# SSD scan with its decays spread over partitions by DMA and joined by predicated copies

## The reference, cut to what matters

```python
cs = jnp.cumsum(dtg * a_neg.astype(f32).reshape(g, r), axis=2)
decay = jnp.exp(jnp.where(causal, cs[:, :, :, None] - cs[:, :, None, :], -jnp.inf))
cb = jnp.einsum("bcign,bcjgn->bcijg", cg, bg)
xdt = dtg[..., None] * xg
y_diag = jnp.einsum("bcijgr,bcjgrp->bcigrp", cb[..., None] * decay, xdt)
y_off = jnp.einsum("bcign,bcgrpn->bcigrp", cg, starts) * jnp.exp(cs)[..., None]
...
y = y_f + y_b[:, ::-1] + lw["ssd_d"][:, None] * xs
```

## Time and profile before

| | |
|---|---|
| median of 3 runs | 3470.36 us (3469.86 to 3471.82) |
| profiled execution, its own time | 3470.05 us |
| its span | 3468.3 us |
| TensorE matmul busy | 3334.0 us (96%) |
| VectorE, ScalarE, GpSimd busy | 1618.2 (47%), 1262.5 (36%), 575.9 us (17%) |
| DMA | 212.96 MB, mean 61 GB/s |
| granted TensorE clock, mean | 0.985 |

### The profile page before, as it was taken

How to read it: one execution, slowest core, us unless ns; L and a number is a source line. 1 busy time by engine, 2 the same in 40 slices (tenths; PEclk the granted TensorE clock), 3 DMA queues, 4 the chain that set the end, 5 groups by cost and what they waited for, 6 DMA issues and landing times. The chain is left out here.

```text
span 3468.3 us, 55579 instructions
## 1 busy us (share of the span) xinstructions
PE 3334.0 (96%) x19856; PEld 3184.6 (92%) x19856; DVE 1618.2 (47%) x2846; ACT 1262.5 (36%) x2383; POOL 575.9 (17%) x703
## 2 busy tenths in 40 slices
PE   7879999999999999999999999899989999999997
PEld 2379999999999999999999998899988999999997
DVE  2373665745736657458366442344334222322233
ACT  4434444545355445443454443221233111110112
POOL 0002332421423324214223240000110000000000
PEclk9999999999999999999999999999999999999998
DMA  8311111111111111111111123443321111111111
GB/s 316 122 31 26 56 43 31 46 43 34 42 43 56 43 28 48 43 33 40 46 51 39 32 83 100 146 137 100 86 71 37 42 43 43 42 42 42 43 35 74
DMA packets 284847, 212.96 MB, mean 61 GB/s; under 512 B 10152, under 2 KB 266576, under 8 KB 284624
## 3 DMA queue, kind: packets, MB, share of 16 engines
q1 hardware_dynamic: 239808, 159.74, 15.3%
q10 hardware_dynamic: 44816, 50.35, 4.8%
HBM read 173.87 MB, written 36.18 MB: 61 GB/s over the span
## 5 line engine op out<-in xcount | busy, mean ns | idle before, releaser
L675 PE MATMUL bank<-h_hi,w_hi 128*128 128x384 f32 (+1 forms) x2520 | 876.7, 348 | 42.0 <-DVE z_t L1290 19.1
L675 PE MATMUL bank<-h_hi,w_lo 128*128 128x384 f32 (+1 forms) x2520 | 846.3, 336 | 0.0
L675 PE MATMUL bank<-h_lo,w_hi 128*128 128x384 f32 (+1 forms) x2520 | 846.3, 336 | 0.0
L1832 PE MATMUL bank<-a_hi,v_hi 128*128 128x384 f32 x1440 | 491.1, 341 | 31.7 <-DVE v_lo L1933 11.9
L675 PEld LDWEIGHTS bank<-h_hi,w_hi 128*128 128x128 f32 (+1 forms) x2520 | 474.4, 188 | 50.4 <-DVE z_t L1290 19.5
L1832 PE MATMUL bank<-a_lo,v_hi 128*128 128x384 f32 x1440 | 485.8, 337 | 0.0
L1832 PE MATMUL bank<-a_hi,v_lo 128*128 128x384 f32 x1440 | 485.7, 337 | 0.0
L675 PEld LDWEIGHTS bank<-h_lo,w_hi 128*128 128x128 f32 (+1 forms) x2520 | 474.7, 188 | 3.6
L675 PEld LDWEIGHTS bank<-h_hi,w_lo 128*128 128x128 f32 (+1 forms) x2520 | 473.5, 188 | 1.2
L1656 POOL TENSOR_TENSOR kq<-kq,fg 128x384 f32<-128x384 f32 x288 | 283.3, 1014 | 435.9 <-PE bank L807 434.6
L1832 PEld LDWEIGHTS bank<-a_hi,v_hi 128*128 128x128 f32 x1440 | 273.4, 190 | 46.8 <-issue 34.7
(11 more groups left out here) (253 smaller groups left out, 4655.3 us busy)
## 6 DMA issues: line engine op xcount, KB each, us to landing
raw<-in_w_in SPq DMA_DIRECT2D x104, 512.0 KB, 3.9
raw<-in_ffn_w SPq DMA_DIRECT2D x60, 512.0 KB, 3.7
ada<-in_ada_w SPq DMA_DIRECT2D x12, 2048.0 KB, 9.3
small<-gate_scratch ACTq DMA_DIRECT2D x72, 192.0 KB, 2.4
gate_scratch<-th ACTq DMA_DIRECT2D x48, 192.0 KB, 1.9
y_scratch<-x_t SPq DMA_DIRECT2D x8, 1152.0 KB, 4.4
small<-y_scratch ACTq DMA_DIRECT2D x48, 192.0 KB, 2.5
raw<-in_w_ssd_out SPq DMA_DIRECT2D x16, 512.0 KB, 4.0
```

The costliest lines, as they stand in the source:

```text
L675: last = pe.matmul(out, w[i][:, k, 0:cols_n], h[:, k, blk(hb)], start=(k == 0 and j == 0), stop=(k == KT - 1 and j == 2))
L1832: last = pe.matmul(banks[3 * s + b][:, 0:BW], wp[s][:, k, :], operand[ap][:, k, blk(b)], start=(k == 0 and j == 0), stop=(k == kt - 1 and ...
```

## The change

The cumulated decays go once, in the prologue, to a scratch in DRAM (18 stores). Per chunk SP loads the eight rows of the group, 4 KB, into all 128 partitions of `cumb` (three buffers). VectorE caps each row at the partition's own cumulated value (`min`), so that the masked side can't overflow; ScalarE makes the exponentials in place; VectorE copies the backward direction over the forward one where the mask says so, and the sum of the two directions' dt on the diagonal, and multiplies by C B straight from the bank. TensorE's decay arguments and GpSimd's sum go. x and B are turned once: `xb` holds all nine chunks. The dt factor's logarithm stays in the bias, the subtraction of `cum` moves to GpSimd per group, exp(cum) to ScalarE per group and into the evacuation of `dec`. Two weight tiles of the next group are loaded ahead of the HGRN state's store, one behind. In the diff "..." marks what is left out.

```diff
+        cum_dram = nc.dram_tensor("cum_scratch", [G, NC, 2, HPG, P], F32, kind="Internal").ap()
...
-        xb = [sb(f"xb{i}", [P, 512], F32, ssd_scope) for i in range(4)]
+        xb = sb("xb", [P, NC, BW], F32, ssd_scope)
         xp = sb("xp", [P, 2, GW], F32, ssd_scope)
         t_off = sb("t_off", [P, 512], F32, ssd_scope)
         y_tok = t_off[:, 0:GW]
-        me = sb("me", [P, 2048], F32, ssd_scope)
-        mm = me[:, 0:1024].rearrange("p (e n) -> p e n", e=2)
-        ex = me[:, 1024:2048]
-        rstd = me[:, 2048 - T:2048]
+        mm = sb("mm", [P, 2, 512], F32, ssd_scope)
+        cumb = sb("cumb", [P, 3, 8 * P], F32, ssd_scope)
+        rstd = cumb[:, :, :].rearrange("p a n -> p (a n)")[:, 0:T]
...
+    reset = acc[1][:, :]
     dt_v, dt_a, dt_b, dt_c, dt_d, dt_e = f_t, g_t, kf_t, kb_t, q_t, s_t
-    cum = x_t[0:64, 0, :]
+    cum = g_t[0:64, :]
...
-            def stage_a(g, tiles):
-                for t in tiles:
-                    base, step = A_COLS[t]
-                    load(g, t, g * step + base)
+            def load_a(g, t):
+                base, step = A_COLS[t]
+                load(g, t, g * step + base)
+
+            def load_cum(g, c):
+
+                if c >= 3:
+                    sp.wait_ge(m_ready.sem, m_ready.at(g, c - 2))
+                src = cum_dram[g:g + 1, c] if isinstance(g, int) else cum_dram[bass.ds(g, 1), c]
+                sp.dma_start(cumb[:, c % 3, :], src.rearrange("a d h t -> a (d h t)").broadcast_to([P, 8 * P])
+                             ).then_inc(cum_in[c % 3], 16)
+
+            def stage_a(g):
+                for t in (2, 3, 4):
+                    load_a(g, t)
+                load_cum(g, 3)
+                load_a(g, 5)
+                for c in (4, 5, 6):
+                    load_cum(g, c)
...
+                if t == 4:
+                    sp.wait_ge(cum_done, 1)
+                    for d in range(2):
+                        for c in range(NC):
+                            sp.dma_start(cum_dram[:, c, d], cum[32 * d:32 * d + 32, chunk(c)]).then_inc(cum_stored, 16)
...
+            sp.wait_ge(cum_stored, 16 * 2 * NC)
+            for c in range(3):
+                load_cum(0, c)
+            load_a(0, 0)
+            load_a(0, 1)
+
             with sp.Fori(0, G - 1) as g:
-                stage_a(g, late)
+                stage_a(g)
                 for t, (base, step) in enumerate(B_COLS):
+                    if t == 1:
+                        load_cum(g, 7)
+                        load_cum(g, 8)
                     if t == 3:
                         stores(g, False)
+                        for c in range(3):
+                            load_cum(g + 1, c)
                     load(g, 6 + t, g * step + (base + step))
+                load_a(g + 1, 0)
+                load_a(g + 1, 1)
                 store_h(g)
-                stage_a(g + 1, early)
...
-            def turn_xb(c, bank, with_cb):
+            def turn_xb(c, bank):
                 for e in range(2):
-                    last = pe.transpose(bank[:, e * P:(e + 1) * P], x_t[:, e, chunk(c)], ident)
-                last = pe.transpose(bank[:, GW:GW + P], b_t[:, chunk(c)], ident)
-                if with_cb:
-                    last = pe.matmul(bank[:, GW + P:GW + 2 * P], b_t[:, chunk(c)], c_t[:, chunk(c)],
-                                     start=True, stop=True)
-                return last
+                    pe.transpose(bank[:, e * P:(e + 1) * P], x_t[:, e, chunk(c)], ident)
+                return pe.transpose(bank[:, GW:GW + P], b_t[:, chunk(c)], ident)
 
             def ssd(g, k):
                 if k == 0:
@@ -696,39 +726,28 @@
                     last.then_inc(tr_ready.sem, 1)
                 if k < NB:
                     pe.wait_ge(silu_done.sem, silu_done.at(g, k - 2))
-                if k < NA1P:
+                if k < 5:
 
                     if k > 0:
                         pe.wait_ge(tr_kept.sem, tr_kept.at(g, 2 * k + 1))
-                    turn_xb(8 - 2 * k, S[0], False).then_inc(tr_ready.sem, 1)
-                    if k < 3:
-                        turn_xb(7 - 2 * k, S[1], False).then_inc(tr_ready.sem, 1)
+                    turn_xb(8 - 2 * k, S[0]).then_inc(tr_ready.sem, 1)
+                    if k < 4:
+                        turn_xb(7 - 2 * k, S[1]).then_inc(tr_ready.sem, 1)
                 if 2 <= k < 2 + NA1P:
                     p = k - 2
                     pe.wait_ge(xp_ready.sem, xp_ready.at(g, p + 1))
                     if p > 0:
                         pe.wait_ge(ctb_used.sem, ctb_used.at(g, p))
                     for j in range(2 if p < 3 else 1):
-                        last = pe.matmul(S[2][:, j * GW:(j + 1) * GW], xb[2 * (p % 2) + j][:, GW:GW + P],
+                        last = pe.matmul(S[2][:, j * GW:(j + 1) * GW], xb[:, 8 - 2 * p - j, GW:GW + P],
                                          xp[:, j, :], start=True, stop=True)
                     last.then_inc(ctb_ready.sem, 1)
                 if 4 <= k < 4 + NC:
                     c = k - 4
-                    pe.wait_ge(tr_kept.sem, tr_kept.at(g, 8 + c))
-                    turn_xb(c, S[0], True).then_inc(tr_ready.sem, 1)
-                    if c > 0:
-                        pe.wait_ge(exp_ready.sem, exp_ready.at(g, c))
-                    else:
-                        pe.wait_ge(sel_ready, g + 1)
-                    for d in range(2):
-                        pe.matmul(S[3 + d][:, :].rearrange("p (h i) -> p h i", i=P), id_bf[:, :],
-                                  neg_bf[d][:, :].rearrange("p (a i) -> p a i", a=1).broadcast_to([P, HPG, P]),
-                                  start=True, stop=False, skip_group_check=True)
-                        for h in range(HPG):
-                            last = pe.matmul(S[3 + d][:, h * P:(h + 1) * P], sel[:, d * HPG + h, :],
-                                             cum_hl[:, chunk(c)], start=False, stop=(h == HPG - 1),
-                                             skip_group_check=True)
-                    last.then_inc(arg_ready.sem, 1)
+                    if c >= 2:
+                        pe.wait_ge(m_ready.sem, m_ready.at(g, c - 1))
+                    pe.matmul(S[3 + c % 2][:, 0:P], b_t[:, chunk(c)], c_t[:, chunk(c)], start=True,
+                              stop=True).then_inc(cb_ready.sem, 1)
...
-            for a, src in enumerate((dt_d, dt_e, dt_b)):
+            for a, src in enumerate((dt_d, dt_e, cum)):
                 for c in range(NC):
                     i = a * NC + c
                     pe.transpose(S[i // 8][:, (i % 8) * 64:(i % 8 + 1) * 64], src[0:64, chunk(c)],
                                  ident[0:64, 0:64])
+            for c in range(NC):
+                pe.matmul(S[4][:, c * 32:(c + 1) * 32], dt_c[0:64, chunk(c)], cst[0:64, K_FOLD:K_FOLD + 32],
+                          start=True, stop=True)
             flat = v_tok[0:64, :, :].rearrange("p c t -> p (c t)")
-            for j in range(2):
-                last = pe.matmul(S[4 + j][:, 0:288], ones[0:64, :], flat[:, j * 288:(j + 1) * 288],
-                                 start=True, stop=True)
+            pe.matmul(S[3][:, 192:480], ones[0:64, :], flat[:, 0:288], start=True, stop=True)
+            last = pe.matmul(S[5][:, 0:288], ones[0:64, :], flat[:, 288:576], start=True, stop=True)
...
-                if 1 <= k < 1 + NA1P:
+                if 1 <= k < 6:
                     p = k - 1
-                    if p >= 2:
-                        wait(ctb_ready, g, p - 1)
-                    for j in range(2 if p < 3 else 1):
+                    for j in range(2 if p < 4 else 1):
                         wait(tr_ready, g, 2 + 2 * p + j)
-                        act.activation(xb[2 * (p % 2) + j][:, 0:BW], S[j][:, 0:BW],
-                                       ACT.Copy).then_inc(tr_kept.sem, 1)
+                        act.activation(xb[:, 8 - 2 * p - j, :], S[j][:, 0:BW], ACT.Copy).then_inc(tr_kept.sem, 1)
+                if k == 3:
+                    act.wait_ge(grp_ready, g + 1)
+                    act.activation(tok_g[:, 2, :, :], tok_g[:, 3, :, :], ACT.Exp)
                 if 5 <= k < 5 + NC:
                     c = k - 5
-                    wait(tr_ready, g, 9 + c)
-                    if c < 4:
-                        wait(ctb_ready, g, 3 if c < 2 else 4)
-                    else:
-                        wait(y_ready, g, c - 3)
-                    act.activation(xb[c % 4][:, :], S[0][:, :], ACT.Copy).then_inc(tr_kept.sem, 1)
-                    wait(arg_ready, g, c + 1)
-                    if c == 0:
-                        act.wait_ge(grp_ready, g + 1)
-                    else:
-                        wait(sum_ready, g, c)
-                    for d in range(2):
-                        for h in range(HPG):
-                            o = d * 512 + h * P
-                            last = act.activation(ex[:, o:o + P], S[3 + d][:, h * P:(h + 1) * P], ACT.Exp,
```

(74 more changed lines are left out.)

71 lines of the change are left out of this document (35 added, 36 removed).

## The result

| | before | after |
|---|---|---|
| median | 3470.18 us (4 runs) | 3413.19 us (3411.3 to 3413.49, 4 runs) |
| ratio, 95% interval | | 0.9834 [0.9817, 0.9851] |
| span of the profiled execution | 3468.3 us | 3411.7 us |
| TensorE clock, mean | 0.985 | 0.981 |

The kernel is 57 us faster. Forecast were 99, and the range ended at 3400: the time lies 13 us above it. So 42 us of the forecast gain are missing, and the profile has to show where.

What follows compares the result with a forecast made beforehand. The prediction took TensorE's own work to bound the mixers. Its terms, -89.3 - 18.5 + 10.4 - 2.6 + 1.5 = -98.5 us from 3470.05, gave a forecast of 3371 us, range 3355 to 3400.

Steps and rivals of the forecast that it cites:

- Terms 1 and 2: TensorE in the mixers: decay arguments leave it (89.3 us) and seven transposes a group go (18.5 us), together 107.8 us.
- term 2: TensorE's transposes of x and B: nine a group go, slots 3 and 4 get one more each, 18.5 us saved.
- Term 3: VectorE's added work makes it lag in slots 8 to 12; TensorE waits in slots 11 and 12, +10.4 us.
- Term 4: ScalarE's exponentials between cap and merge: shorter chain, cover of about 1 us, so cost 0.
- the sign that the prediction had named for being wrong: At VectorE's merge: the prediction is wrong if ScalarE's exponentials are what the merge waits for.
- Term 5: New 512 KB decay loads on SP, tight at chunks 4 and 7: just fit, cost 0, ends 0 and 32 us.
- Term 6: Prologue's dt chain: -2.6 us for a shorter chain, +1.5 for added small products and evacuation; ends 0 and 5 us.
- C: Waits of A or B bring TensorE's clock down once a group, 21 us on top of B: about 3415; chance 0.04.
- D: Broadcast loads of one row crawl at caps of chunks 4 and 7: slower than before, 3507 at 14 us; chance 0.03.
- E: Arguments filled time TensorE would have waited; idle appears in slots 4 to 6, 3400 to 3460 us; chance 0.02.
- A: VectorE sets the pace outright in slots 8 to 12, 24 us more: 3395; chance 0.17.
- B: Loads of chunks 4 and 7 land 1 to 2 us late, 16 to 32 us: 3387 to 3403; chance 0.10.

Runs made afterwards that it cites:

- e7: Kernel before without the ten decay-argument matmuls of each chunk on TensorE, ScalarE's exponentials run as tanh: 3377.02 us, ratio 0.973.
- e8: Kernel before without the second transposes of x and B in slots 4 to 12, product of B and C kept: 3445.03 us, ratio 0.9929.
- e5: Kernel of e3 with one of VectorE's two predicated copies left out, the one that brings in the backward direction: 3368.11 us, ratio 0.9704.
- e11: Kernel of e10 with VectorE's cap ahead of the merge in each slot, not behind it: 3384.08 us, ratio 0.9752.
- e10: Kernel of e2 with SP holding chunk 6's load until chunk 4 is merged instead of chunk 3: 3384.69 us, ratio 0.9757.
- e1: Changed kernel with the loop's edge at slot 3 instead of slot 9, SP's list unchanged: 3410.42 us, ratio 0.9831 to the kernel before.
- e3: Kernel of e2 with the loop's edge also moved from slot 9 to slot 3: 3393.27 us, ratio 0.9782.
- e4: Kernel before with the loop's edge at slot 3 instead of slot 9, for SP too: 3482.5 us, ratio 1.0041.
- e2: Changed kernel with loads of chunks 4 and 5 ahead of weight tile 5, chunk 7's ahead of stage B's first tile: 3386.59 us, ratio 0.9764.
- e9: Kernel before plus three unused 512 KB copies, held until VectorE made chunk 3's product so they run across the loop's edge: 3495.34 us, ratio 1.0076.

## Why the prediction was wrong

- **Terms 1 and 2** (107.8 us off TensorE): right. e7 and e8 measured 92.4 and 24.4 us for what was worked out as 89.3 and 23.8 (term 2 gives 16 of 72 sets back in slots 3 and 4). By the slots' period, 6.81 for 6.87.
- **Term 3** (VectorE's lag, 10.4 us): the mechanism was right, the size 16.8. The step that was mis-sized is "out of slots 5 to 7 about 0.5 late": the y products of slot 8 already waited 1.08 us in all eight groups, and slot 12 again 0.66, where the prediction had slots 11 and 12. The merges of slots 5 to 7 wait 1.2 to 1.4 us for exponentials, and two caps in that stretch took 1.50 and 1.67 us instead of 1.22. VectorE's new operations in a slot also took 0.2 us more than the sum had (1.62 for 1.5, 1.29 for 1.22). And the 2.1 us a group of these waits aren't the whole price: where no long wait at slot 9 hides it, it is some 3 us (25 us in e5, over eight groups).
- **Term 4** (ScalarE's chain, cost 0): wrong in slots 5 to 7. The cover of 1 us was worked out for a slot with a y part in it; slots 5 to 7 have none or a short one, so the merge comes early in VectorE's list and the exponentials, which can't start before the cap at the end of the slot before, are late: 31.5 us of waits, the sign that the prediction had named for being wrong. With the cap first (e11 against e10) the merges' waits fall to 8.9 us and the wait of slot 8 is gone; with one copy less (e5) it is gone as well, while the merges wait as before. So either cure is enough for slot 8, and the late exponentials cost TensorE nothing by themselves. The step from bank to SBUF was right in size: eight take 2.45 us, where the earlier trace rows have 2.18.
- **Term 5** (loads, taken as 0, ends 0 and 32): the landing was right, the lateness at VectorE 10.7 us over all. This was the step that failed, but not by its bounds: it asked only who waits for the loads and what is queued behind them on SP. It didn't ask what else uses the DMA engines at that moment. The six waits "for nothing that the profile shows" were in the prediction as 6.0 us that stay or go. They were instruction fetches at the loop's back edge, and the change puts 2 MB of loads in front of them. 26.2 - 6.0 = 20 us of waiting, and 12 us for the clock behind the six waits: 32 of the 42 us missed. The rest is term 3. These are what stands in this trace and not what each repair gives back: halving the edge's waits alone gave 3 us (e1), since the lag came out instead.
- **Term 6** (prologue): first idle 16.7 us for 16.5 forecast, the second 2.8 for 2.9.
- **Rivals.** C had the fall of the clock, at the wrong place and with the wrong cause. D and E didn't come; the loads of one row 128 times took 3.6 to 4.2 us alone, where a weight tile takes 3.9. A and B came in part, but no rival has a wait for instructions, so the range had no place for it. That C's 3415 is close to the measured 3413 is luck: it has falls behind late loads of chunks 4 and 7, in eight groups and 2.6 us each, and the trace has them at six edges, 1.5 to 2.9 us each.

The sum by what was measured (the nine small products of the prologue, at most 1.1 us, weren't measured and are left out): -92.4 - 19.0 (56 x 0.34) + 16.8 (VectorE) + 20.2 (edge) + 11.7 (clock) - 2.4 + 0.3 (prologue) = -64.8, against -57.0. Most of the 7.8 us left over can be placed. A slot in which the y products wait is 0.17 us longer than the listed wait explains (slot 8: 8.06 for 6.81, listed 1.08), 20 times, 3.4 us. And at the end of the mixers TensorE is 58.9 us ahead of the kernel before (e7: 90.8), so some 2 us on each side come from the rest of the program, which no edit touches.

The Trainium skill ("Runtime: NRT & Kernel Launch", section on instruction fetch mechanics) says that the sequencer fetches instructions through a DMA queue of its own, and that a taken branch to a page it doesn't hold forces a fetch before execution goes on. The traces agree: the packets of q8 and q14 stand in each of these waits, which come six times for a loop of seven passes. It calls the cost of crossing a block in sequence mostly hidden and has no figure for a taken branch. Here the taken branch cost 1.0 us with quiet queues, and 4.4 us with 2 MB of loads around it.

What stays open: whether the weight tile whose transfer ends just ahead of the edge (by 0.4 us in e1, e3 and e4, by 1.2 us in e10) makes the waits of some 2 us at slot 3 (e1, e3, e4, e5) and in e2 and e10; the table says so, no run tests it by itself. Nor is it known why the clock fell behind 17 of these 36 waits and not behind the others, which are no shorter.

## What to carry to other kernels

Rows of waits with no cause are a resource too: find out what they are before moving DMA traffic next to them. A DMA share read during a wait is not enough; read the stretch ahead of it too. When a kernel has a hardware loop, look where its back edge stands, and keep bulk loads from running across it or up to it; SP's order alone was worth 27 us here. An engine that follows in lockstep has to be followed slot by slot from the first slot with new work, since its lag starts where the slots are short.

## What the runs showed of the hardware

- The clock can fall behind a wait shorter than the prologue's 2.5 us. In e11 TensorE idled 1.72 us at 1003.7 and was granted 0.55 from 1007 to 1010:

```profile
985.40:988.00 2.60, 2.57 (x15) 2.58 (x16) 0.84 (x2) 1.82 (x7) 0.00 (x0) 1.00 0.05 13
...
1007.00:1010.00 3.00, 3.00 (x11) 2.44 (x10) 2.81 (x5) 2.45 (x8) 0.61 (x1) 0.55 0.28 111
1010.00:1014.00 4.00, 4.00 (x25) 4.00 (x24) 3.90 (x10) 0.01 (x1) 0.01 (x1) 1.00 0.00 0
```

  while after the 1.08 us at its edge it stayed at 1.00. The fall cost 1.7 us, so a wait of that size can cost its own length once more. It doesn't always: of the six waits of 1.5 to 1.9 us in e11 four brought the clock down, and the longest, 1.88 us, didn't. Behind most edges a fall cost 1.5 to 1.7 us, at the most 3.1 (e9).
- VectorE's cap, one operation with two inputs in SBUF, took 1.22 us in most of its 72 places and up to 1.67 where GpSimd worked at the same time:

```profile
975.59 1.22 DVE L1377 TENSOR_TENSOR cumb<-cumb,tok_g 128x1024 f32<-128x1024 f32 x1
...
981.71 1.50 DVE L1377 TENSOR_TENSOR cumb<-cumb,tok_g 128x1024 f32<-128x1024 f32 x1
...
988.14 1.67 DVE L1377 TENSOR_TENSOR cumb<-cumb,tok_g 128x1024 f32<-128x1024 f32 x1
```

```profile
975.67 2.36 POOL L1631 TENSOR_TENSOR xp<-xb,tok_g 128x256 f32<-128x256 f32 x2
981.52 0.61 POOL L1631 TENSOR_TENSOR xp<-xb,tok_g 128x256 f32<-128x256 f32 x1 [3.49 <-PE bank L769]
988.11 0.61 POOL L1631 TENSOR_TENSOR xp<-xb,tok_g 128x256 f32<-128x256 f32 x1 [5.98 <-PE bank L775]
```

  The second and third of these caps run beside a GpSimd product of 0.61 us, and are longer by 0.28 and 0.45. The first overlaps GpSimd too, at 975.67, and isn't, so the overlap alone doesn't settle it; it wasn't tried by itself.
